# Second block's first products from the uncentred sum, turned modulation rows ahead of the last gate half, rotary tables on GpSimd

## What is computed

```python
# end of each layer of the first block
f = square(relu(h @ mlp_w1[i])) @ mlp_w2[i]
e = sigmoid(h @ ple_w_gate[i]) * (p[i] @ ple_w_proj[i])
x = layer_norm(DN_ALPHA * h + f + e, ln2_g[i], ln2_b[i])
# begin of each layer of the second block
mod = silu(c) @ w_ada + b_ada                 # 6 * 1024 values for each layer
shift1, scale1, gate1, shift2, scale2, gate2 = split(mod, 6)
h = rms_norm(x, norm1_g) * (1 + scale1) + shift1
p = h @ w_in                                  # retention, RWKV and convolution columns
cos, sin = cos(positions * inv_freq), sin(positions * inv_freq)   # rotary tables
```

## Time and profile before

| | |
|---|---|
| median of 3 runs | 2348.4 us |
| the profiled execution, its span | 2348.21 us, 2346.4 us |
| TensorE busy | 2217.2 us, 94% of the span |
| VectorE, ScalarE, GpSimd busy | 984.0, 464.2, 310.7 us |
| mean granted TensorE clock | 0.991 |

### The profile page before, as it was taken

The page is one execution under the profiler, slowest core; times in us unless marked ns, Lnnn a source line. Parts: engine busy times, 40 slices in busy tenths (PEclk is TensorE's granted clock), DMA queues, the critical chain, the costliest instruction groups (busy, mean ns, idle before and its releaser), DMA issues.

```text
span 2346.4 us, 33634 instructions
## 1 busy us (share of the span) xinstructions
PE 2217.2 (94%) x14458; PEld 1525.2 (65%) x14458; DVE 984.0 (42%) x1816; ACT 464.2 (20%) x1061; POOL 310.7 (13%) x259
## 2 busy tenths in 40 slices
PE   9999999999999999999888888899999999888888
PEld 8777777687768899997333333388999863333333
DVE  5588855468856666533100000065755230000001
ACT  3422213622214321312000000043113020000001
POOL 2300002210003055500000000012454000000000
PEclk9999999999999999999999999999999999999999
DMA  7287742278752433359999999944243899999997
GB/s 281 98 330 281 285 183 95 100 277 306 299 195 81 145 122 115 109 227 401 427 428 428 428 427 428 411 166 146 91 145 109 318 408 428 428 427 428 428 425 311
DMA packets 136864, 654.94 MB, mean 279 GB/s; under 512 B 9864, under 2 KB 15112, under 8 KB 108168
## 3 DMA queue, kind: packets, MB, share of 16 engines
q1 hardware_dynamic: 136712, 652.72, 70.1%
HBM read 651.64 MB, written 1.05 MB: 278 GB/s over the span
## 4 chain that ended last, share of the span: by engine, by line
PE 76%; DMA 18%; DVE 2%; ACT 2%; SPq 1%; issue 1%; POOL 0%; DVEq 0%; ACTq 0%; POOLq 0%
PE bank L853 75%; DMA ring<-in_w_exp_up 12%; DMA PRGT<-in_w_exp_up 5%; ACT R L3621 1%; SPq L767 1%; DMA PRGT<-in_w_exp_down 1%; PE bank L1538 0%; DVE sm L2286 0%; POOL PRGT L3719 0%; ACT SQ L3661 0%; PE bank L1039 0%; DVE PRGT L2838 0%; ACT PRGT L3437 0%; DVE PRGT L2280 0%; DVE PRGT L2843 0%
## 5 line engine op out<-in xcount | busy, mean ns | idle before, releaser
L853 PE MATMUL bank<-hT,ring 128*128 128x256 f32 (+1 forms) x2288 | 402.7, 330 | 0.0
L853 PEld LDWEIGHTS bank<-hT,ring 128*128 128x128 f32 x2288 | 357.9, 191 | 62.4 <-issue 14.3
L853 PE MATMUL bank<-PRGT,R 128*32 128x512 f32 (+1 forms) x1152 | 275.7, 594 | 33.3 <-DMA PRGT<-in_w_exp_up 19.5
L853 PE MATMUL bank<-ring,R 128*32 128x512 f32 (+1 forms) x992 | 253.2, 594 | 38.6 <-DMA ring<-in_w_exp_up 23.4
L853 PE MATMUL bank<-PRGT,ring 128*128 128x256 f32 (+6 forms) x1520 | 254.4, 354 | 1.2 <-ACT PRGT L3156 0.8
L853 PEld LDWEIGHTS bank<-PRGT,ring 128*128 128x128 f32 (+3 forms) x1520 | 214.1, 177 | 35.1 <-issue 4.2
L853 PEld LDWEIGHTS bank<-PRGT,R 128*32 128x32 f32 (+1 forms) x1152 | 77.8, 113 | 193.9 <-issue 192.9
L853 PE MATMUL bank<-PRGT,SQ 128*32 128x512 f32 (+2 forms) x864 | 191.4, 530 | 13.0 <-ACT SQ L3661 12.2
L853 PEld LDWEIGHTS bank<-ring,R 128*32 128x32 f32 (+1 forms) x992 | 70.4, 115 | 169.4 <-issue 168.7
L853 PE MATMUL bank<-ring,SQ 128*32 128x512 f32 (+2 forms) x640 | 167.4, 519 | 8.4 <-ACT SQ L3661 8.3
L853 PE MATMUL bank<-PRGT 64*64 64x64 f32 (+3 forms) x1584 | 145.4, 263 | 4.3 <-issue 1.4
(11 more groups left out here) (482 smaller groups left out, 2816.8 us busy)
## 6 DMA issues: line engine op xcount, KB each, us to landing
PRGT<-in_w_exp_gate SPq DMA_DIRECT2D x42, 2048.0 KB, 32.1
ring<-in_w_exp_up SPq DMA_DIRECT2D x36, 2048.0 KB, 31.9
ring<-in_mlp_w SPq DMA_DIRECT2D x32, 2048.0 KB, 9.4
PRGT<-in_w_exp_down SPq DMA_DIRECT2D x30, 2048.0 KB, 31.0
PRGT<-in_w_exp_up SPq DMA_DIRECT2D x28, 2048.0 KB, 31.9
PRGT<-in_w_ada SPq DMA_DIRECT2D x32, 1536.0 KB, 8.8
ring<-in_w_exp_down SPq DMA_DIRECT2D x24, 2048.0 KB, 33.6
ring<-in_w_exp_gate SPq DMA_DIRECT2D x22, 2048.0 KB, 32.2
```

Of the source, the lines that this page charges most:

```text
L853: return mm(o, lhsT=lhsT, rhs=rhs, start=first, stop=last, **kw)
```

## The change

- `AHEAD` of layer 1 holds gain * R, not centred. It gets a third extra column, the gain itself, so that PSUM also holds the weights' sum over the gains; VectorE multiplies that by the negative mean (`MINUS_MEAN`), adds it and multiplies by the reciprocal of the norm's root, for all four tiles at once and ahead of the second norm's reciprocal. `first_tiles` keeps only what follows.
- ScalarE writes tiles 0 to 5 of `AHEAD` between its squares, VectorE tiles 6 and 7 ahead of `layer_norm`. GpSimd's `center` waits in layer 1 until all are written. In layer 0 `AHEAD` stays centred.
- TensorE's order, in both layers: three gate pairs, the twelve modulation sums, the first half of the last gate pair, `turn_rows` (twelve products, each a 128x128 piece of a modulation row as weights with 4 columns, into `acc[0]`; the transposes and their banks go), the second half. Then in layer 1 `block_first(0, 3)` (12 products), `norm_of_sum`, `block_first(3, 8)` (20 products) and 8 idle products, and only `rms_norm` stands between these and `dense`. In layer 0 `norm_of_sum` follows at once, with 3 idle products.
- SyncE's load of the second block's third weight block waits for the first pairs' last bank, as before (now bank 0 of the four).
- GpSimd computes the rotary tables, ahead of its part of layer 1's second norm, in 24 chained instructions of 256 columns; VectorE no longer does.

```diff
+            def block_first(k0, k1):
+                n, W = BANK_AT["first0"], slot(2, KT)
+                if k0 == 0:
+                    pe.wait_ge(slot_full[2], loaded(SLOT_AT["mid_even0"][0][1]))
+                for k in range(k0, k1):
+                    pe.wait_ge(sems["ahead_in"], KT + k + 1)
+                    for c in (1, 2, 3, 0):
+                        if k == 0:
+                            pe.wait_ge(bank_read[(n + c) % BANKS], emptied(n + c))
+                        ins = mul(bk(n + c)[:, 0:S + 3], W[:, k, c * P:(c + 1) * P], AHEAD[:, k, :], k == 0, k == KT - 1)
+                        ...
...
-                norm_of_sum((sems["norm_in"], L.nxt("norm_in", 4)))
-                t0 = BANK_AT[f"ada_t{l}"]
-                for q in range(3):
-                    ...
-                        ins = nc.tensor.transpose(bk(t0 + q)[:, j * P:(j + 1) * P],
-                                                  ADA_ROW[:, q * 512 + j * P:q * 512 + (j + 1) * P], C("ident"))
-                idle_products(acc[0], 3)
+                def turn_rows():
+                    pe.wait_ge(sems["norm_in"], in0 - 3)
+                    for q in range(3):
+                        pe.wait_ge(bank_read[(a0 + q) % BANKS], filled(a0 + q))
+                        for j in range(4):
+                            ins = mul(acc[0][:, 16 * q + 4 * j:16 * q + 4 * j + 4], ADA_ROW[:, q * 512 + j * P:q * 512 + (j + 1) * P],
+                                      C("ident")[:, 0:P:32])
+                    ins.then_inc(sems["down_turned"], 1)
+                in0, n = L.nxt("norm_in", 4), n0 + 3
+                pe.wait_ge(bank_read[n % BANKS], emptied(n))
+                for h in range(2):
+                    for k in range(KT):
+                        ins = mul(bk(n)[:, h * S:(h + 1) * S], W[:, k, (2 + h) * P:(3 + h) * P], hT[:, k, :], k == 0, k == KT - 1)
+                    if h == 0:
+                        turn_rows()
+                ins.then_inc(bank_full[n % BANKS], 1)
+                if l:
+                    block_first(0, 3)
+                norm_of_sum((sems["norm_in"], in0))
+                if l:
+                    block_first(3, KT)
+                    idle_products(acc[1], 8)
+                else:
+                    idle_products(acc[1], 3)
...
-                    first_two_pairs(0, 5, range(4))
                     rms_norm()
-                    for j in range(2):
-                        first_two_pairs(5, KT, (2 * j, 2 * j + 1))
... VectorE, second block, layer 0
-                    rotary_tables()
+                    for c in (1, 2, 3, 0):
+                        dve.wait_ge(bank_full[(n0 + c) % BANKS], filled(n0 + c))
+                        ins = v.tensor_copy(at(c), bk(n0 + c)[:, S:S + 3])
+                    stepped(ins)
+                    for c in range(4):
+                        v.scalar_tensor_tensor(PR[:, 28 + c, :], MINUS_MEAN, at(c)[:, 2:3], bk(n0 + c)[:, 0:S], ALU.mult, ALU.add).then_inc(
+                            bank_read[(n0 + c) % BANKS], 1)
+                    for c in range(4):
+                        dve.wait_ge(bank_read[(n0 + c) % BANKS], filled(n0 + c))
+                        ins = v.tensor_tensor(PR[:, 28 + c, :], PR[:, 28 + c, :], stat[:, 1, :], ALU.mult)
+                    stepped(ins)
... ScalarE
                 gate(0)
+                gate(1)
                 for j in range(3):
-                    gate(j + 1)
                     square(j)
-                ada_row(0)
+                    if l:
+                        ahead(2 * j, 2 * j + 1)
+                    if j == 1:
+                        gate(2)
+                        for q in range(3):
+                            ada_row(q)
+                gate(3)
                 square(3)
-                ada_row(1)
-                ada_row(2)
```

More of the change, by code:

```diff
@@ L425, in build @@
         QRAW, QSIN, QCOS = R[:, 0:4, :], R[:, 4:8, :], hT[:, 0:4, :]
-        AHEAD = flat(PR[:, 0:9, :])[:, 0:KT * (S + 2)].rearrange("p (k n) -> p k n", k=KT)
+        AHEAD = flat(PR[:, 0:9, :])[:, 0:KT * (S + 3)].rearrange("p (k n) -> p k n", k=KT)
+        MINUS_MEAN = hsum3[:, 0:S]
         FF = PR[:, 32:40, :]
@@ L1245, in ffn_and_ple @@
                             pe.wait_ge(sems["combined"], 8 * l + 3)
+                        if b == 1 and j == 1:
+                            break
                         pair(n0 + 2 * b + j, lambda h, k: W[:, k, (2 * j + h) * P:(2 * j + h + 1) * P], lambda k: hT[:, k, :], KT)
@@ L1415, in first_pair @@
                                 ins.then_inc(bank_full[(n0 + h) % BANKS], 1)
[L1417 to L1425, removed]
                 if l:
                     rms_norm_ahead()
[L1429 to L1432, removed]
+                    for h in range(2):
+                        pe.wait_ge(bank_read[(n0 + h) % BANKS], emptied(n0 + h))
+                    pe.wait_ge(slot_full[2], loaded(SLOT_AT[f"mid_even{l}"][0][1]))
                     first_pair(0, KT)
                 else:
-                    first_two_pairs(0, 5, range(4))
                     rms_norm()
-                    for j in range(2):
-                        first_two_pairs(5, KT, (2 * j, 2 * j + 1))
                 ready = normed(KT)
@@ L2447, in ffn_and_ple @@
                 dve.wait_ge(sems["norm_in"], L.nxt("norm_in", 4))
-                t0 = BANK_AT[f"ada_t{l}"]
                 def modulation():
[L2452 to L2462, removed]
+                    if l:
+                        v.tensor_scalar(MINUS_MEAN, stat[:, 0, :], -1.0, None, ALU.mult)
+                    dve.wait_ge(sems["down_turned"], L.nxt("down_turned"))
+                    stepped(v.tensor_tensor(mod[:, 48 * l:48 * l + 48].rearrange("p (q j b) -> p q j b", q=3, j=4),
+                                            acc[0][:, 0:48].rearrange("p (q b j) -> p q j b", q=3, b=4),
+                                            V_(f"b_ada{l}").rearrange("p (q j b) -> p q j b", q=3, j=4), ALU.add))
                 def ahead(k):
@@ L2475, in ahead @@
                         dve.wait_ge(sems["ahead_in"], KT * (l + 1))
[L2477 to L2481, removed]
+                if l:
+                    dve.wait_ge(sems["ahead_in"], KT * l + ACT_AHEAD)
+                    for m in range(ACT_AHEAD, KT):
+                        v.tensor_scalar(AHEAD[:, m, 0:S], R[:, m, :], gain[:, m:m + 1], None, ALU.mult).then_inc(sems["ahead_in"], 1)
+                layer_norm(l == 0, modulation, None if l else ahead)
             attention("dsa", 4, 0, DSA_D ** -0.5, [2.0 ** (-8.0 * (h + 1) / DSA_H) for h in range(DSA_H)])
@@ L3340, in ada_row, with ahead, centred_ahead @@
                     copy_out(BANK_AT[f"ada{l}"] + q, ADA_ROW[:, q * 512:(q + 1) * 512])
+                gain = sm[:, AG:AG + KT] if l else V_("ln2_g0")
+                def ahead(*tiles):
+                    for k in tiles:
+                        f(AHEAD[:, k, 0:S], R[:, k, :], ACT.Copy, scale=gain[:, k:k + 1]).then_inc(sems["ahead_in"], 1)
+                def centred_ahead():
+                    for j in range(ACT_AHEAD // 2):
+                        act.wait_ge(sems["norm_centered"], 8 * l + 4 + j + 1)
+                        ahead(2 * j, 2 * j + 1)
                 gate(0)
+                gate(1)
                 for j in range(3):
-                    gate(j + 1)
                     square(j)
-                ada_row(0)
-                square(3)
-                ada_row(1)
-                ada_row(2)
[L3350 to L3358, removed]
+                    if l:
+                        ahead(2 * j, 2 * j + 1)
+                    if j == 1:
[3 more added lines that the diff above has]
+                gate(3)
+                square(3)
+                layer_norm(xT, f"ln2_g{l}", f"ln2_b{l}", beside=None if l else centred_ahead)
             attention(4, 0, DSA_D ** -0.5, 4)
@@ L3735, in norms @@
                 i0 = L.nxt("norm_in", 4) - 4
-                for ready in (lambda q: (bank_read[(m0 + q) % BANKS], filled(m0 + q)), lambda q: (sems["norm_in"], i0 + q + 1)):
+                for r, ready in enumerate((lambda q: (bank_read[(m0 + q) % BANKS], filled(m0 + q)), lambda q: (sems["norm_in"], i0 + q + 1))):
+                    if r and mixer == "mla_out":
+                        rotary_tables()
                     sq = L.nxt("norm_sq", 4) - 4
@@ L3746, in norms @@
                     nc.gpsimd.tensor_tensor(both(0), both(0), both(2), ALU.add).then_inc(sems["presummed"], 1)
+                    if r and mixer == "mla_out":
+                        pool.wait_ge(sems["ahead_in"], 2 * KT)
                     center(sq)
```

59 lines of the change are left out of this document (23 added, 36 removed).

## The result

The kernel after takes 2363.45 us (median of 4 runs, 2361.4 to 2363.63) against 2348.27 us before (4 runs beside it, 2347.51 to 2349.2): ratio 1.0061, 95% interval [1.0048, 1.0074], +15.2 us. Forecast was +9.1. The profiled execution took 2363.5 us with a span of 2361.6, also 15.2 more than before.

The account below looks back on a forecast made before the run. TensorE itself was taken to bound the kernel, DMA far behind. Layer 1's seam, +6.7 us, and layer 0, +2.4, sum to +9.1 on the profiled 2348.21: 2357.3, or 2357.5 for the median; range 2348.5 to 2362.5.

Parts of the forecast that it names:

- turn_rows: Between the last gate pair's halves: twelve narrow products add 2.2 us in each layer, bounds 1.8 and 3.3.
- a rival with the chance 0.12: Seam, layer 1: the clock falls behind TensorE's idle stretch, 0.61 granted over 3.7 us, 1.4 us lost; 2358.9 us; chance 0.12.
- The hole: Layer 1, between `rms_norm` and `dense`: no first products left to cover the norm's latency, TensorE idle, +3.76 us.
- ScalarE's pace: Layer 1, `dense`: TensorE follows ScalarE's `hT` tiles, 0.505 us each against 0.435 a product, +0.5 us.
- The lower bound: `turn_rows`: second record 0.31 - 0.24 = 0.07 us after the first, 24 records, 1.8 us.
- The idle products in full: Layer 1, ahead of `rms_norm`: eight idle products end after the squares, hide in no wait, +3.45 us.
- Layer 0: End of layer 0: mean starts 2.6 us later, plus 3.05 to the first `AHEAD` tile, less 3.27; +2.4 us.
- The waits of 0.48 and 1.11: Layer 0, around the norm's sums: two TensorE waits, costing 0.6 and 1.1 us of the layer's sum.
- the lower of my ends: Layer 0, VectorE's addition into `R`: 0.7 us taken, or 1.65 beside GpSimd's square sum, that end adding 0.9.
- GpSimd's tables at nothing: Rotary tables on GpSimd: 24 instructions at no more than 1.04 us, 25 us, done before needed; cost nothing.
- The stages behind swallow nothing: Expert stages: the delay passes on, as SyncE's loads wait for engines; the opposing rival said 2348.4 us, chance 0.13.
- The range's upper end: 2362.5 us, given as the forecast's own upper end, 2360.6, with the clock's price.

Follow-up runs that it names:

- e2: The kernel before plus only twelve unread four-column products between the halves of the last gate pair, in both layers; 2356.85 us, ratio 1.0039.
- e3: The kernel after without the eight idle products ahead of the second block's `rms_norm`; 2360.24 us, ratio 1.005.
- e4: The kernel after with layer 1's first products reordered: 4 before the norm's sums, 20 behind, 8 behind `rms_norm`, no idle products; 2357.32 us, ratio 1.0038.
- e6: The kernel after with layer 0 of the first block back in the order of before, layer 1 as changed; 2357.67 us, ratio 1.004.
- e1: The kernel after with the twelve narrow products issued one at a time between products of the last gate pair, both layers; 2360.53 us, ratio 1.0052.
- e7: The kernel after with twelve 128-column transposes in place of the narrow products, same place, both layers; 2357.55 us, ratio 1.0039.
- e5: The kernel before with only the rotary tables moved from VectorE to GpSimd; 2347.86 us, ratio 0.9997.
- e8: The kernel before with tables on GpSimd, layer 1's `AHEAD` uncentred and no idle products there, TensorE's old order otherwise; 2345.77 us, ratio 0.9986.

## Why the prediction was wrong

The direction was right, and so were the steps of the order, the waits and the idle products. The size fell short by 6.1 us, and 4.8 of them are there because the forecast kept the clock at its upper level.

- **The failed step is the clock, which the sum puts at nothing.** Every product of 256 columns behind `turn_rows` and behind the hole is priced at the full rate. The only place for a fall was a rival with the chance 0.12: one event at the hole, set against the mean of 0.991 over the span, which says nothing of one stretch. It happened there, and I never asked for it at `turn_rows`, because TensorE is not idle there. Even that rival's 2358.9 us is 4.5 too low. A fall behind the narrow run costs 5.23 - 3.48 = 1.75 us, with eight products at 0.435 as the measure. The profiled execution has both: 3.5 us. Over all profiles with the compact run the half pair behind it was slow 6 times in 9 (after 2 of 2, e2 1 of 2, e3 2 of 2, e4 1 of 2, e6 0 of 1); with the products spread (e1) or transposes in their place (e7) 0 times in 4, and where nothing interrupts the pair (both layers of before, e5 and e8, layer 0 of e6) 0 times in 7.
- **The hole.** Its length was right, 3.69 against 3.76. Behind it I gave 0.5 us for ScalarE's pace; `dense` took 8.83 instead of 7.07, 1.76. Following tile by tile at half clock replaces the pacing, it is not added to it. The rival's price for the clock, 1.4, was near the 1.3 that `dense` took beyond e4's 7.50, but partly by luck: the profiles with the hole show 8.61 to 10.14 for `dense`, 1.1 to 2.6 beyond it. The slow stretch came in every profile with the hole (after, e1, e3, e6, e7) and not in e4. The Trainium skill ("TensorE: Matmul & The Clock Gate", HAM oscillation) says that after a long wait between bursts the next burst starts cold. These rows agree (3.69 us of idle time, 5 of 5). The mistake was to weight it by the mean clock, which hides it.
- **`turn_rows`** was 2.60 us a layer, not 2.2: 0.108 for each record, as near as can be to the 0.109 of a transpose's one record, and inside the bounds of 1.8 and 3.3. The weight loads fill the stretch (PEld busy 2.59 of 2.60 us). The lower bound was misread: 0.31 - 0.24 takes the mean of two records of unequal length (0.20 and 0.28). In the trace the second starts 0.03 us behind the first and the next product 0.11 behind the second, 0.14 for the whole product; why it is quicker than the 0.217 here is not shown. The Trainium skill (same page, LDWEIGHTS) puts a load at its columns over 1.2 GHz, for 128 columns an estimate of 107 ns; the 0.108 agree. Two layers: 0.8 us.
- **The idle products in full**, +3.45: right, 749.04 to 752.49, and e3 gives 3.2 back.
- **Layer 0**: 2.4 forecast, 5.09 in the trace. 0.4 and 1.75 are the two terms above. 0.2 is a slip in the sum: the pair ends 2.82 + 2.2 later and the mean starts 3.4 instead of 5.60 behind it, which is 2.8 later and not 2.6. The waits of 0.48 and 1.11 are as forecast, and 0.3 is left in the latencies. VectorE's addition took 0.69, the lower of my ends.
- **GpSimd's tables at nothing**: right, e5. The bound of 1.04 us for each instruction was not: the cast took 1.42 and two others 1.07. All 24 took 21.8 us, inside the 25.
- **The stages behind swallow nothing**: right. `lora` starts 14.87 us late (768.56 against 753.69), the end 15.2.

The sum with the measured sizes: 9.1, + 0.2 (the slip), + 0.8 (`turn_rows`), + 3.5 (two falls), + 1.3 (`dense` behind the hole beyond the 0.5), + 0.4 (what is left in the latencies of both layers) = 15.3; less the 0.36 by which this execution was ahead before the change begins, 14.9 of 15.2 us. The range's upper end has a slip too: 2360.6 and 1.4 are 2362.0, not 2362.5; the measured time lies outside either.

Open is what decides whether a narrow run is followed by a fall. The same instructions in the same kernel (e2, e4) did and did not show it. The range of the kernel after, 2361.4 to 2363.63, is about as wide as one fall, but the executions without a profile do not show their windows, and their mean clock does not follow their time (e2's slowest, 2358.38 us, has the highest, 0.991). Open is also what it is in the run that matters: e7 changed the columns (4 to 128) and the number of records (24 to 12) at once.

## What to carry to other kernels

Before a step of TensorE is made "smaller", count its weight loads: twelve products of 4 columns cost twice the twelve transposes that they replaced, and the full-rate products behind them ran at half clock in most profiled cases. Price the granted clock stretch by stretch, behind a hole of this length (3.7 us here) and behind a run of narrow products, and do not let the span's mean talk you out of it. Of the products that can cover the latency of a norm, keep some behind its last sum; idle products in front of it buy nothing.

## What the hardware did that I had not expected

- The granted clock fell from 1.00 to 0.50 directly behind 2.60 us in which TensorE had issued without a gap (24 records of 128x4), and came back within about 4 us. Idle time is not needed for a fall.
- A float32 product of 4 columns costs 0.217 us, two records at 0.108, whether alone between products of 256 columns (e1: 0.22) or in a run. A transpose of 128 columns costs 0.109. This is not so everywhere: the product of 32 columns in the earlier trace rows took 0.14 us to the next one.
- The fall at the hole is not tied to the moment at which work begins again. In the kernel after the clock is still 1.00 in the first 0.5 us of `dense` (759.80 to 760.30); in e6 it is down in the last 1.6 us of the hole, with TensorE idle; e1 and e7 show it in the hole too. The window of e6:
```profile
752.00:753.60 1.60, 0.00 (x0) 0.00 (x0) 1.56 (x5) 0.70 (x2) 0.00 (x0) 0.51 0.00 0
```
